# Weight layers of a transformer block: from a ring of two whole tiles to a ring of four half tiles

## The reference, cut to what matters

```
p = h @ w_in                                    # 2048 x 16448, tokens and context
o = bidirectional_deltanet(qkv, ab, ...)        # chunked gated delta rule
y = (g_conv * (conv @ w_conv_out) + g_dn * (o @ w_dn_out)) @ w_out
x = x + mod[2] * y
q = h @ w_q                                     # scores, top 16 of 128 x 128 experts per head
x = x + mod[5] * (sum over the chosen experts: gelu(h . u_tab[e]) * v_tab[e])
p2 = h2 @ w_in_2                                # second mixer: three branches
out = rms_norm(x + sum_b gate_b * (branch_b @ w_out_2[b]))
mod = silu(c) @ w_mod + b_mod                   # six modulation rows, 2048 x 12288
```

## Time and profile before

| | before |
|---|---|
| median of 3 runs | 4309.7 us (4304.96 to 4316.59) |
| profiled execution: its time / its span | 4311.87 us / 4310.1 us |
| granted TensorE clock, mean | 0.986 |
| TensorE busy | 4149.6 us (96%) |
| VectorE / ScalarE / GpSimd busy | 2995.6 / 1957.6 / 222.8 us |
| DMA | 846.28 MB, mean 196 GB/s |

### The profile page before, as it was taken

One profiled execution on the slowest core, in us unless ns is written; L12 is line 12 of the kernel. 1 busy time (PEld: TensorE's weight loads), 2 busy tenths in 40 slices (PEclk: granted clock), 3 DMA queues, 4 the chain that ended last, 5 costly groups with the idle time before them and its releaser, 6 DMA issues. The chain is left out here.

```text
span 4310.1 us, 65526 instructions
## 1 busy us (share of the span) xinstructions
PE 4149.6 (96%) x24351; PEld 3581.8 (83%) x24351; DVE 2995.6 (70%) x5129; ACT 1957.6 (45%) x2942; POOL 222.8 (5%) x532
## 2 busy tenths in 40 slices
PE   8999999899989999899999999999999999999999
PEld 1788888779988999788888887778787888888889
DVE  5777885866786677578866665566666567876746
ACT  1542223537643334444455554444444454454644
POOL 0000000000016600000000000000000100300000
PEclk9999999999999999999999999999999899999999
DMA  9673433468774357556655555666666444444454
GB/s 373 232 266 126 156 137 118 153 221 280 260 221 123 106 216 261 178 191 210 209 187 178 183 184 203 233 234 236 231 236 240 144 166 171 148 166 153 170 195 157
DMA packets 213845, 846.28 MB, mean 196 GB/s; under 512 B 67808, under 2 KB 105968, under 8 KB 126464
## 3 DMA queue, kind: packets, MB, share of 16 engines
q1 hardware_dynamic: 213632, 843.37, 56.4%
HBM read 792.85 MB, written 50.45 MB: 196 GB/s over the span
## 5 line engine op out<-in xcount | busy, mean ns | idle before, releaser
L2649 PE MATMUL bank<-rounded,rounded 128*128 128x512 f32 x2048 | 737.0, 402 | 7.6 <-DVE rounded L2795 7.6
L3520 PE MATMUL bank<-rounded,rounded 128*128 128x512 f32 x1856 | 668.0, 403 | 11.2 <-DVE rounded L3764 8.0
L2651 PE MATMUL bank<-rounded,rounded 128*128 128x256 f32 x2048 | 574.2, 280 | 0.0
L3521 PE MATMUL bank<-rounded,rounded 128*128 128x256 f32 x1856 | 521.0, 281 | 0.0
L251 DVE TENSOR_TENSOR rounded<-arena,rounded 128x1024 fp32r<-128x1024 f32 x255 | 312.0, 1224 | 289.1 <-ACT rounded L244 288.9
L2649 PEld LDWEIGHTS bank<-rounded,rounded 128*128 128x128 f32 x2048 | 386.0, 188 | 94.7 <-issue 8.3
L244 ACT ACTIVATE rounded<-arena 128x1024 fp32r<-128x1024 f32 x255 | 270.3, 1061 | 411.6 <-PE bank L3047 377.3
L2703 ACT ACTIVATE rounded<-arena 128x1024 fp32r<-128x1024 f32 x256 | 271.5, 1061 | 371.4 <-PE bank L2651 368.2
L3520 PEld LDWEIGHTS bank<-rounded,rounded 128*128 128x128 f32 x1856 | 349.9, 189 | 101.2 <-issue 15.2
L3764 DVE TENSOR_TENSOR rounded<-arena,rounded 128x1024 fp32r<-128x1024 f32 x230 | 283.4, 1232 | 196.2 <-ACT rounded L3566 194.6
L3045 PE MATMUL bank<-rounded,rounded 128*128 128x512 f32 x1024 | 405.6, 396 | 12.1 <-DVE rounded L251 9.1
(11 more groups left out here) (516 smaller groups left out, 9271.8 us busy)
## 6 DMA issues: line engine op xcount, KB each, us to landing
arena<-in_w_in SPq DMA_DIRECT2D x244, 1024.0 KB, 4.9
arena<-in_peer_u SPq DMA_DIRECT2D x128, 1024.0 KB, 5.1
arena<-in_peer_v SPq DMA_DIRECT2D x128, 1024.0 KB, 4.9
arena<-in_w_mod SPq DMA_DIRECT2D x80, 1024.0 KB, 7.6
arena<-in_w_out SPq DMA_DIRECT2D x40, 1024.0 KB, 4.9
arena<-in_w_conv_out SPq DMA_DIRECT2D x16, 1024.0 KB, 5.0
arena<-in_w_dn_out SPq DMA_DIRECT2D x16, 1024.0 KB, 4.9
arena<-in_peer_w_q SPq DMA_DIRECT2D x16, 1024.0 KB, 5.9
```

The costliest lines, as they stand in the source:

```text
L2649: pe.matmul(k.ps[r][:], wh, flat(k.r(pair_slot + 2 * kt, 2)), start=(kt == 0), stop=False, skip_group_check=True)
L2651: mm = pe.matmul(k.ps[r][:, 0:L], wl, k.r(pair_slot + 2 * kt, 1)[:, 0, :], start=False, stop=(kt == KT - 1), skip_group_check=True)
L3520: pe.matmul(both, wh, hi_lo(kt), start=(kt == 0), stop=False, skip_group_check=True)
L3521: mm = pe.matmul(one_, wl, hi(kt), start=False, stop=(kt == KT - 1), skip_group_check=True)
```

## The change

All weight layers get a ring of four half tiles in the same 32 slots. A half tile is loaded by a DMA of its own (`load_tile`, 128 x 1024, 512 KB) into its quarter of slots 0 to 15; the high part goes to its own quarter of slots 16 to 31; **the low part is written over the loaded weights**. With four pairs instead of two, ScalarE's hi no longer waits for TensorE, only for the half tile's landing. In return the load of half q of tile j waits for `half_done` >= 2(s+j-2)+1+q: TensorE must be done with the half four before. `load_next` does so for the first two tiles of the next stage, `query_stage`'s two loads for `conv_stage` wait for `half_done` instead of `lo_done`, and `expert_output` issues its piece of `w_mod_gate2` (and does its `add_row`) earlier in each group of four tiles. Functions that no stage calls (`split`, `linear3`, `channel_norm`, `elementwise`, `save`, `load_raw`) are removed. The matmuls, their order and the conversions' sizes stay.

```diff
@@ Core
-        self.raw_loaded = [sem(f"weights_in_raw{r}") for r in range(2)]
+        self.raw_loaded = [sem(f"weights_in_half{r}") for r in range(4)]
...
-    def staged(self, part, b):
-
-        return self.r(16 + 8 * b + 4 * part, 4).rearrange("p s c -> p (s c)")
+    def raw_half(self, tile, q):
+
+        return flat(self.t(8 * (tile % 2) + 4 * q, 4))
+
+    def staged(self, part, tile, q):
+
+        return flat(self.r(8 * (tile % 2) + 4 * q + (0 if part else 16), 4))
...
-def make_high(k, act, g, r, q, s, first):
-
-    b, c = q, slice(q * 1024, (q + 1) * 1024)
-    if q == 0:
-
-        act.wait_ge(k.raw_loaded[r % 2], g * 32 + (16 * ((s + r) // 2) + 16))
-    if not (first and r == 0):
-
-        act.wait_ge(k.half_done, g * (2 * SLOTS) + (2 * (s + r) + q - 1))
-    act.activation(k.staged(0, b), k.raw(r % 2)[:, c], ACT.Copy).then_inc(k.hi_done, 1)
+def make_high(k, act, g, r, q, s):
+
+    act.wait_ge(k.raw_loaded[2 * (r % 2) + q], g * 32 + (16 * ((s + r) // 2) + 16))
+    act.activation(k.staged(0, r, q), k.raw_half(r, q), ACT.Copy).then_inc(k.hi_done, 1)
 
 
 def make_low(k, dve, g, r, q, s):
 
-    c = slice(q * 1024, (q + 1) * 1024)
     dve.wait_ge(k.hi_done, g * (2 * SLOTS) + (2 * (s + r) + q + 1))
-    dve.tensor_tensor(k.staged(1, q), k.raw(r % 2)[:, c], k.staged(0, q), ALU.subtract).then_inc(k.lo_done, 1)
+    dve.tensor_tensor(k.staged(1, r, q), k.raw_half(r, q), k.staged(0, r, q), ALU.subtract).then_inc(k.lo_done, 1)
+
+
+def load_tile(k, sp, w, r, need):
+
+    for q in range(2):
+        if need is not None:
+            sp.wait_ge(k.half_done, need + q)
+        sp.dma_start(k.raw_half(r, q), w[:, q * 1024:(q + 1) * 1024]).then_inc(k.raw_loaded[2 * (r % 2) + q], 16)
+
+
+def load_next(k, sp, following, s_end):
+
+    for r in range(2):
+        load_tile(k, sp, following[r], r, 2 * (s_end - 2 + r) + 1)
...
@@ first_stage, and alike in every other stage
             for j in range(2, tiles):
-                sp.wait_ge(k.lo_done, 2 * (s + j - 2) + 2)
-                sp.dma_start(k.raw(j % 2), w[j]).then_inc(k.raw_loaded[j % 2], 16)
+                load_tile(k, sp, w[j], j, 2 * (s + j - 2) + 1)
...
@@ query_stage
             for r in range(2):
-                sp.wait_ge(k.lo_done, 2 * (s + tiles - 2 + r) + 2)
+                sp.wait_ge(k.half_done, 2 * (s + tiles - 2 + r) + 2)
                 sp.dma_start(k.raw(r), w_next[r]).then_inc(k.plain_loaded[r], 16)
...
@@ expert_output
+            sp.dma_start(rows, k.i["w_mod_gate2"][0]).then_inc(rows_in, 16)
             for r in range(2, SLOTS):
                 load(0, r)
                 acts_in(0, r + 2)
-            sp.dma_start(rows, k.i["w_mod_gate2"][0]).then_inc(rows_in, 16)
...
-                    if r == 2 * SLOTS - 1:
+                    if r == SLOTS:
                         sp.wait_ge(row_added, g + 1)
...
+                    if r == 1:
+                        add_row(g, half)
```

More of the change, by code:

```diff
@@ L247, in make_low @@
 def make_low(k, dve, g, r, q, s):
-    c = slice(q * 1024, (q + 1) * 1024)
     dve.wait_ge(k.hi_done, g * (2 * SLOTS) + (2 * (s + r) + q + 1))
-    dve.tensor_tensor(k.staged(1, q), k.raw(r % 2)[:, c], k.staged(0, q), ALU.subtract).then_inc(k.lo_done, 1)
[L254 to L262, removed]
-    if tiles > SLOTS:
-        with sp.Fori(1, tiles // SLOTS) as g:
-            for r in range(SLOTS):
-                load(w[bass.ds(g * SLOTS + r, 1)].rearrange("a p n -> (a p) n"), r,
-                     g * (2 * SLOTS) + (2 * (s + r - 2) + 2))
@@ L491, in _ @@
                 for m in range(8):
-                    wh, wl = (k.staged(p, q)[:, m * P:(m + 1) * P] for p in range(2))
+                    wh, wl = (k.staged(p, j, q)[:, m * P:(m + 1) * P] for p in range(2))
                     kt = 8 * q + m
@@ L2309, in _ @@
             low(HEADS - 2)
-def elementwise(k, name, ops):
-    with ExitStack() as stage:
-        finished = k.sem(stage, f"{name}_finished")
-        block = stage.enter_context(k.nc.Block())
-        @block.vector
-        def _(dve):
-            for op in ops:
-                op(dve).then_inc(finished, 1)
 def output_stage(k, weights, o_hi, o_lo, br_slot, y_slot, x_slot, following3, x_saved):
@@ L3143, in add_row, with group @@
                 ins.then_inc(row_added, 1)
-            def group(g, last, first=False):
+            def group(g, half, last, first=False):
                 for r in range(SLOTS):
@@ L3515, in _ @@
                 for m in range(8):
-                    wh, wl = (k.staged(p, half)[:, m * P:(m + 1) * P] for p in range(2))
+                    wh, wl = (k.staged(p, j, half)[:, m * P:(m + 1) * P] for p in range(2))
                     kt = 8 * half + m
```

310 lines of the change are left out of this document (50 added, 260 removed).

## The result

The changed kernel takes 4344.46 us (median of 4 runs, 4338.71 to 4351.96) against 4307.82 us before: ratio 1.0083, 95% interval 1.0068 to 1.0099. It is slower by 0.8%, above the range of 4280 to 4340. The profiled execution is the fastest of the four, 4338.71 us, so the two traces can account for 26.8 of the 36.6 us between the medians.

A forecast was written before the change was run, and what follows sets the result against it. TensorE, busy 4149.6 of 4310.1 us, was taken as the bound, leaving only idle time to win. -27.8 + 19 + 8.5 + 5 = +4.7 us on the profiled execution gave 4314 us by median, no change; range 4280 to 4340.

The forecast's parts named there:

- pieces of `w_mod` decide: Slower rival: in first_stage and output_stage each piece 2.5 us late, each such wait followed by half clock; 4341 us, chance 0.19.
- The lead: Conversions running ahead in the weight stages remove TensorE's waits for low parts: 27.8 us won, bounds 15 to 40.
- SP waits longer, and everything behind it: SP's later load wait delays five w_mod pieces each in first_stage and output_stage: 10 x 1.9 = 19 us lost.
- I take 3.2 - 1.3 = 1.9 us late: Lateness per w_mod piece: issued 3.2 us later, landing 1.3 us sooner; bounds 0.9 and 3.2 us.
- The credit of 1.3 us: Sooner landing of a w_mod piece queued behind 512 KB rather than 1 MB: 1.3 us per piece.
- "covered" pieces: w_mod pieces with even ROW_AT[4n-5], having 2.8 us more slack, so their lateness was expected to cost nothing.
- The clock: Half clock for 3.4 us behind half of ten new TensorE waits: 5 x 1.7 = 8.5 us lost, bounds 0 and 17.
- Other work behind loads: Small blocks, expert_input's activations, the mixers store and delta_prepare's end come later: 5 us lost, bounds 0 and 15.
- Free of charge: Some 570 more DMAs on SP, half-tile transfers and the low part written over loaded weights: no cost taken.
- Loads don't overlap: Rival: a tile takes 7.6 instead of 5.7 us in stages of 16 or 24 matmuls per half; some 5430 us, chance 0.01.
- the lead does not form: Rival: ScalarE's evacuations and VectorE's joins tie the conversion to where it is, nothing won; 4342 us, chance 0.06.
- Faster: Rival: conversions running ahead take in nearly all waits and w_mod pieces land at the early bound; 4285 us, chance 0.28.

The follow-up runs named there:

- the fastest one: Changed kernel with w_mod pieces ahead of half loads, delta_prepare's transfers half a tile earlier, x and x_saved transfers in 512 KB parts; 4276.61 us, ratio 0.9936.
- experiment 3: Changed kernel in which the high part of half h again waits until TensorE is done with half h-2; 4375.40 us, ratio 1.0164.
- experiment 12: The fastest one, with the high part waiting for TensorE as before the change; 4311.71 us, ratio 1.0011.
- Experiment 2: Kernel before, with SyncE waiting until TensorE is done with half 2j-3 ahead of each w_mod piece in first_stage and output_stage; 4315.72 us, ratio 1.0016.
- experiment 1: Changed kernel with w_mod pieces in first_stage and output_stage issued ahead of both half loads of their tile; 4296.82 us, ratio 0.9977.
- experiment 5: Changed kernel with each w_mod piece in first_stage and output_stage issued between its tile's two half loads; 4305.67 us, ratio 0.9996.
- Experiment 11: Changed kernel with only delta_prepare's row loads, matrix stores and delta_aq stores one half earlier in SyncE's order; 4335.26 us, ratio 1.0067.
- experiment 8: Changed kernel with w_mod pieces ahead of half loads, delta_prepare's transfers half a tile earlier, x transfers in 512 KB parts; 4283.30 us, ratio 0.9935.
- experiment 6: Kernel before, with every weight tile loaded by two 128 x 1024 DMAs one behind the other; 4313.55 us, ratio 1.0018.

## Why the prediction was wrong

The forecast was 4314 us, no change; what came is the rival "pieces of `w_mod` decide" (4341, a chance of 0.19). By the steps:

**The lead: right in sum, partly by luck.** 27.8 us were forecast as won; taking the lead away costs 31 us in the changed kernel and 35 in the fastest one (experiments 3 and 12). Its place was partly wrong. I counted only waits that the trace lists, 7.0 us in `expert_output` and 6.0 in `mixers`; they won 14.2 and 11.5, since matmuls also follow each other faster when the low part is there early (of the 14.2, 10.3 are busy time, experiment 3). `delta_prepare`, of which 6.6 were forecast, gave nothing. Two errors of place cancel in the sum.

**SP waits longer, and everything behind it: right in kind, too small; this is the step that failed.** The pieces n = 3, 6, 9, 11 and 14 were named, and behind these the five large waits of each stage stand. The term that was mis-sized is "I take 3.2 - 1.3 = 1.9 us late". The credit of 1.3 us for half the bytes ahead of the piece measured 0.3 (median landing 6.8 against 7.1 us): the other half tile comes into the queue while the piece is in flight, and both flights move about the same, 2.3 MB before (315 GB/s over 7.45 us) and 2.1 MB now. 3.2 - 0.3 = 2.9 us is also what TensorE shows: its waits behind the ten pieces rose from 3.1 to 32.8 us, 3.0 per piece, against 1.9. All idle time of the two stages rose by 30.7 us, or 34 with the 3.1 of gain that I had put there. The 4 us beyond the ten are mainly "covered" pieces, which show too, with three waits of around 1 us. Experiment 2 delays the piece as much, but the load in front is then 3.3 us old; it cost 8 us, near my lower bound of 0.9 apiece. Experiments 1 and 5 show that the place in the queue gives the loss back. (In the same paragraph half of 2.6 us is 1.3, not 1.4; nothing hangs on it.)

**The clock: mis-sized with it.** I took half of ten waits with 1.7 us each, 8.5 us. At eight of the ten large waits the granted clock falls to the lower level, at three of these over about 6.8 instead of 3.4 us, and TensorE's busy time in the two stages rose by 12.0 us.

**Other work behind loads: incomplete.** 5 us were forecast. The wait behind the small blocks rose from 3.86 to 5.02 us (2.2 forecast) and the one at `expert_input`'s end from 4.46 to 6.37 (1.4 forecast). I missed `delta_prepare`'s stores of `delta_aq`, which also moved behind SP's later wait: their three waits of 1.8 us took what I had counted as gain, and the stage went to +4.6 instead of -3.9. Experiment 11 takes 8.9 us off the stage. In `branch_outputs`, costed at nothing, the 2 MB load behind tile 2 makes a new wait of 1.76 us; experiment 8 removes it. `expert_input` (+3.5) has no experiment of its own, and beyond its last wait its growth is open.

**Free of charge: nearly.** Half loads alone cost 7 us in the kernel before (experiment 6), where I had taken none.

**The rivals.** "Loads don't overlap" and "the lead does not form" fell, as expected. "Faster" needed what I didn't see in it: an order of the other transfers that fits the new wait.

The sum with measured terms: lead -31, pieces and clock 34 + 12 = +46, the rest (`delta_prepare`'s stores, blocks, half loads, 2 MB transfers) some +12 by difference, not measured: +27 on the profiled execution. The prediction's own bounds, all taken at their bad end (15 won; 32, 17 and 15 lost), give 4359 us, so the result lies inside them; the range of 4280 to 4340 was too narrow for them.

## What to carry to other kernels

A wait that moves later on a DMA queue is paid by what stands behind it, not by the transfer it guards: list every DMA behind it with its consumer's slack, and move those without slack ahead of the wait, before judging the new buffers. When estimating how much sooner such a transfer lands, count all the bytes that move while it is in flight, and look how long before it the load in front went out: here halving that load won 0.3 us, and 3 us of distance 2.1. And a deeper ring can be worth more than the waits that TensorE's row shows: compare matmuls per microsecond in stretches without idle time, and look at the waits of the weight loads.

## What the runs showed of the hardware that was not expected

TensorE can lose 1.7% with no idle time in its own row: 175 instead of 178 matmuls in 40 us at full clock where the conversions don't run ahead (three kernels without the lead, two with it, in most windows of `expert_output`). Two thirds of it, in the window looked at, are stalls of 0.1 us at a weight load that waits for its low part; the 0.39 us recorded per matmul, at 0.23 us from start to start, cover them. What makes the rest wasn't tried.

A 1 MB load landed in 5.0 us (median) when the load in front of it had gone out 3.3 us earlier, 1.7 MB moving in its flight; in 6.8 with half a tile issued 0.37 us before it and another behind it; in 7.1 to 7.2 with a whole tile issued just before it.

At TensorE's waits of 2.1 to 4.6 us the granted clock fell to 0.50 in eight of ten cases. The length alone doesn't tell which: behind the wait of 2.98 us that ends at 268.76 it stayed at 1.00, behind one of 2.97 us that ends at 1747.50 it was 0.50, and behind one of 2.56 us (211.72) too.
